# Third block's mixer: the attention projection split by heads, a joint root for the layer norm, and heads normalized from one clipped and scaled sum

## The chip, the cores and the metric

One core of a Trainium2 chip runs the whole program. The metric is device microseconds of one execution, the median over runs. TensorE (PE) multiplies, VectorE (DVE), ScalarE (ACT) and GpSimd (POOL) work on tiles of 128 partitions, and SyncE's queue (SP) starts the loads of weights. Every engine works through its own instructions in the order in which they were written, and waits at semaphores for the others.

## The reference

Three blocks run one after another on x of 512 tokens by 1024 features. The change touches only the mixer of the third:

```
h = rms_norm_3(x, mix_norm)
g_a, g_b, z_uv, z_q, z_k, z_v = split(h @ w_in)          # 6144 columns
# branch a: u, v = gelu(z_uv); v = layer_norm(v) * gain + bias (over 512 features, eps 1e-5)
#           y_a = u * (masked 128x128 product of v by chunks + b_s)
# branch b: 8 heads of two query/key parts of 64 and a value of 128
q, k = partial_rope(rms_norm(q)), partial_rope(rms_norm(k))
a = softmax(q1 k1) - lam * softmax(q2 k2)                # causal, blocks of 128 queries
o = rms_norm_3(a @ v, subln) * (1 - lam_init)            # over the head's 128 features, eps 1e-6
m = sigmoid(g_a) * (y_a @ a_w_proj) + sigmoid(g_b) * (y_b @ b_w_proj)
x = x + m @ w_out
```

Around it lie the two gated feed-forward layers of the block. All of it is float32 in precision.

## The kernel before

**Layout.** Activations are kept with features on partitions: a tile `t(i)` is 128 features by 512 tokens. A projection is made of "dense" groups: one group gives 128 output features and runs over its input's k steps (8 for 1024 features). Each k step is three matmuls of 128x128 by 128x512, since weights and inputs are carried as two rounded parts: high by high, high by low, low by high (L863 to L865). A weight panel (up to 8 k steps) is loaded by SP to one of three buffers `W`, its high part is copied by ACT and its low part subtracted by POOL (`split`, L2231 and L2612) into one of four buffers `R`. Inputs are split to two parts likewise by `pair`: ACT copies the high part (L2266), DVE subtracts to the low one (L1484).

**Order.** The order of all steps is a list, `ORDER`, made before the program is written. Each engine's function walks it and issues its own part of each step. Where many small chains run beside projections, `merge(chains, *fills)` builds the list: it keeps a planned clock for each engine from the costs in `SEG`, takes a chain's step as soon as its predecessors (`AFTER`) are planned to be done by the time PE is free, and otherwise takes the next two k steps of a fill. Of several fills the first whose input or tile is free (`room`) is taken. A group once begun is finished before another is opened. A projection's result lies in one of two banks of PSUM in merged stretches, in one of seven in the stretches marked `wide`.

**The mixer of the third block before** (`order`, from L617). After norm 5 come the four `v` tiles of branch a (`gv`, and `gvt`, their transposes to tokens on partitions). Then the three input tiles of head 0 and the three of head 1 are put in the list, outside the merge. Then a merge of three chains: heads 0, 2, 4, 6; heads 1, 3, 5, 7 (`diff_head`); and branch a (`mlp`): per token block m a mean and centering (`gn`, DVE, with ACT's square and sum), then its root and scaling (`gn2`), then four `gu` tiles with `gs` and `pair`. The fills are the inputs of heads 2 to 7, and `rest`: gate tiles of branch a with `a_proj`, and gate tiles of branch b. Inputs of heads 2 and 3 need branch a finished, those of head h from 4 on need head h-4 normalized. Head h starts once head h-2 is normalized (`slot_free`).

A head: transpose v, squares of q and k, token sums on PE (L874), a root of Newton steps on DVE (`newton`, L1378 to L1391), spreads on PE (L888), scaling (L2033, L2036), rotation (`fr`, PE L1354 and L1356, DVE L2172 to L2175), then four query blocks: scores L1314, maximum L2050, exponent L2521, the difference of the two softmaxes L2073 and L2075, transposes L1323, product with v L1332. Its ending is `ft1` to `ft3`: ACT copies the output (L2583); DVE makes a clipped copy and one scaled by 2^-70 (L2185, L2186), ACT squares both, PE sums both over features with a matrix of ones (L1361, L1363), DVE joins the two sums, adds eps and takes the reciprocal (L2197 to L2202), ACT takes the root (L2595), DVE applies a mask and scales the output (L2208, L2210).

After the merge: eight pairs of the heads' outputs, then `b_proj` over all eight k steps of each of 8 groups, each followed by `branch` on DVE (gate times product L1816, add to m L1820), the pairs of m, and `out3` (evicted at L1517) with the next norm's work.

## Time and profile before

| | |
|---|---|
| median of 3 runs | 3356.03 us (3352.72 to 3356.92) |
| the profiled execution's time | 3356.43 us |
| its span, first to last instruction | 3354.6 us |
| PE busy | 3159.9 us, 94% |
| DVE, ACT, POOL busy | 1646.1, 1047.7, 1160.5 us (49%, 31%, 35%) |
| DMA | 22.6% of 16 engines, 74 GB/s |

A profile is one execution. Busy shares are means over the span, so each reading starts from a stretch: what it holds, who is busy in it, and what PE waited for. A window's row gives, after its bounds and length, the busy microseconds of each engine with the number of instructions, then the granted clock of PE as a share of full speed, and the DMA. The mixer of the third block lies between 2400 and 3000 us of the span.

### The profile page before, as it was taken

The page shows a single profiled execution, that of the slowest core. Times are in us where ns is not written, and L with a number is a line of the kernel's source. Part 1 is how long each engine was busy: PE and PEld are TensorE (multiplying, and loading weights), DVE is VectorE, ACT ScalarE, POOL GpSimd, SP SyncE. Part 2 cuts the span into 40 slices and gives each one's busy share as a digit, 9 for nine tenths or more (in the row PEclk, how much of TensorE's full clock was granted, in tenths as well). Part 3 has the DMA queues.
Part 4 walks back from the last instruction along what each step waited for, and adds up shares of the span by engine and source line. Part 5 has one row for each costly group of instructions (what it writes and reads, how often), then busy time and mean ns, then how long its engine had stood idle before and what let it go on. Part 6 is the DMA issues. An engine that isn't in the chain of part 4 may idle for free.

```text
span 3354.6 us, 40426 instructions
## 1 busy us (share of the span) xinstructions
PE 3159.9 (94%) x16604; PEld 2589.4 (77%) x16604; DVE 1646.1 (49%) x3287; ACT 1047.7 (31%) x1691; POOL 1160.5 (35%) x542
## 2 busy tenths in 40 slices
PE   7989999998999898999999989999788999899999
PEld 5768888897888786867877768888666777678887
DVE  4865656454577416557674343331337576443310
ACT  3342223222322223223223333232224334332221
POOL 2442333333444342213212334444322223334443
PEclk9998999999999999999999989999899999899999
DMA  3211111112244331012011222233211112223232
GB/s 113 82 45 38 57 45 63 57 45 72 98 152 144 115 99 54 21 37 67 22 39 49 75 66 94 96 98 99 86 57 55 54 59 73 65 80 100 95 101 88
DMA packets 71480, 247.88 MB, mean 74 GB/s; under 512 B 8064, under 2 KB 8448, under 8 KB 71168
## 3 DMA queue, kind: packets, MB, share of 16 engines
q1 hardware_dynamic: 71296, 245.30, 22.6%
q8 instruction: 131, 2.15, 0.3%
q14 instruction: 53, 0.43, 0.0%
HBM read 243.18 MB, written 2.10 MB: 73 GB/s over the span
## 4 chain that ended last, share of the span: by engine, by line
PE 86%; DVE 11%; ACT 2%; issue 1%; POOL 0%; DMA 0%; SPq 0%; DVEq 0%; ACTq 0%
PE bank L863 22%; PE bank L865 22%; PE bank L864 22%; PE bank L903 7%; PE bank L874 2%; PE bank L897 1%; PE bank L1314 1%; PE bank L881 1%; PE bank L1332 1%; PE bank L888 1%; PE bank L1323 1%; DVE u L1484 1%; DVE sm L1389 0%; PE bank L1160 0%; PE bank L1208 0%
## 5 line engine op out<-in xcount | busy, mean ns | idle before, releaser
L2612 POOL TENSOR_TENSOR R<-W,R 128x1024 fp32r<-128x1024 f32 (+2 forms) x448 | 1050.1, 2348 | 1960.4 <-ACT R L2231 1960.4
L863 PE MATMUL bank<-u,R 128*128 128x512 f32 (+1 forms) x3440 | 1391.8, 405 | 43.3 <-issue 12.4
L865 PE MATMUL bank<-u,R 128*128 128x512 f32 (+1 forms) x3440 | 1355.4, 394 | 0.0
L864 PE MATMUL bank<-u,R 128*128 128x512 f32 (+1 forms) x3440 | 1355.0, 394 | 0.0
L863 PEld LDWEIGHTS bank<-u,R 128*128 128x128 f32 (+1 forms) x3440 | 655.1, 190 | 199.7 <-issue 39.9
L865 PEld LDWEIGHTS bank<-u,R 128*128 128x128 f32 (+1 forms) x3440 | 652.9, 190 | 143.6 <-issue 0.8
L864 PEld LDWEIGHTS bank<-u,R 128*128 128x128 f32 (+1 forms) x3440 | 655.1, 190 | 130.2 <-issue 3.3
L2231 ACT ACTIVATE R<-W 128x1024 fp32r<-128x1024 f32 (+2 forms) x448 | 450.4, 1012 | 197.9 <-PE bank L865 194.8
L903 PE MATMUL bank<-t,t 128*128 128x128 f32 x2000 | 238.8, 276 | 3.5 <-DVE t L1700 1.0
L903 PEld LDWEIGHTS bank<-t,t 128*128 128x128 f32 x2000 | 233.3, 192 | 10.3 <-DVE t L1676 1.8
L2266 ACT ACTIVATE u<-t 128x512 fp32r<-128x512 f32 x126 | 76.3, 627 | 291.7 <-DVE t L1506 246.2
L1517 DVE SCALAR_TENSOR_TENSOR X<-bank,X 128x512 f32<-128x512 f32 x32 | 22.1, 692 | 260.3 <-PE bank L865 260.3
L1492 DVE TENSOR_TENSOR t<-bank,t 128x512 f32<-128x512 f32 x66 | 45.5, 690 | 171.5 <-PE bank L865 158.9
L1484 DVE TENSOR_TENSOR u<-t,u 128x512 fp32r<-128x512 f32 x126 | 98.5, 804 | 51.5 <-ACT u L2266 51.3
L2273 ACT ACTIVATE t<-t 128x512 f32<-128x512 f32 x66 | 41.7, 633 | 243.3 <-DVE t L1492 243.2
L874 PEld LDWEIGHTS bank<-CN,t 128*128 128x128 f32 x672 | 92.3, 213 | 25.5 <-issue 9.4
L874 PE MATMUL bank<-CN,t 128*128 128x1 f32 (+1 forms) x672 | 89.2, 261 | 17.1 <-ACT t L2238 8.0
L1506 DVE TENSOR_TENSOR t<-t,bank 128x512 f32<-128x512 f32 x66 | 45.4, 687 | 120.3 <-PE bank L865 118.6
L1528 DVE SCALAR_TENSOR_TENSOR t<-bank,sm,t 128x511 f32<-128x511 f32 (+2 forms) x108 | 80.8, 748 | 46.5 <-ACT t L2282 43.9
L2638 POOL TENSOR_TENSOR t<-t,CN 128x512 f32<-128x512 f32 x40 | 51.8, 1297 | 114.9 <-PE bank L903 114.8
L2521 ACT ACTIVATE t<-t,sm 128x128 f32<-128x128 f32 (+3 forms) x96 | 53.9, 561 | 116.8 <-DVE sm L2053 116.7
L1816 DVE SCALAR_TENSOR_TENSOR t<-t,bank 128x512 f32<-128x512 f32 x48 | 33.0, 687 | 105.7 <-PE bank L865 105.6
(368 smaller groups left out, 2844.1 us busy)
## 6 DMA issues: line engine op xcount, KB each, us to landing
W<-in_in SPq DMA_DIRECT2D x48, 512.0 KB, 3.3
W<-in_ff_in SPq DMA_DIRECT2D x44, 512.0 KB, 3.4
W<-in_g_qkv SPq DMA_DIRECT2D x24, 512.0 KB, 3.3
W<-in_ada SPq DMA_DIRECT2D x24, 512.0 KB, 3.5
W<-in_f1g SPq DMA_DIRECT2D x22, 512.0 KB, 3.3
W<-in_f1u SPq DMA_DIRECT2D x22, 512.0 KB, 3.3
W<-in_f2g SPq DMA_DIRECT2D x22, 512.0 KB, 3.3
W<-in_f2u SPq DMA_DIRECT2D x22, 512.0 KB, 3.3
```

Source lines behind the costliest of these rows:

```text
L863: e.matmul(b[0:cols, :], wh, hi, start=(k == 0), stop=False)
L864: e.matmul(b[0:cols, :], wh, lo, start=False, stop=False)
L865: i = e.matmul(b[0:cols, :], wl, hi, start=False, stop=(k == KT - 1))
L874: i = e.matmul(b[:, m * n:m * n + n], x[:, m * 128:m * 128 + 128], one, start=first and m == 0, stop=last and m == 3, skip_group_check=True)
L903: i = e.matmul(b[:, s], l[:, s], x[:, s], start=True, stop=True)
L1484: e.tensor_tensor(r(lo[k]), t(src[k]), r(hi[k]).bitcast(F32), SUB).then_inc(*PR.dve.up("lo", tag, k))
L1528: e.scalar_tensor_tensor(out=c[:, s:512], in0=b[:, 0:512 - s], scalar=half(wname, (3 - s) * nt + gj), in1=c[:, s:512], op0=MUL, op1=ADD).t ...
L2231: e.activation(R[q % NH][:, 0:n], W[p % NW][:, 0:n], ACT.Copy).then_inc(*PN.act.up("hi", key))
L2266: e.activation(r(hi[k]), t(src[k]), ACT.Copy).then_inc(*PR.act.up("hi", tag, k))
L2521: e.activation(ex, ex, ACT.Exp, bias=c[:, 0:1], scale=0.125, accum_out=c[:, 1:2]).then_inc(*AT.act.up("exp", u, m, qb))
L2612: e.tensor_tensor(R[q % NH][:, 1024:1024 + n], W[p % NW][:, 0:n], R[q % NH][:, 0:n].bitcast(F32), SUB).then_inc(*PN.pool.up("lo", key))
L2638: e.tensor_tensor(v3(t(V_.d)), v3(t(V_.L)), C(f"q{16 << n}").unsqueeze(1).broadcast_to([128, 4, 128]), MUL).then_inc(*IV.pool.up("q", v, n))
```

## The change

**Order.** The inputs of heads 0 and 1 go from the fixed list into the first fill. The layer norm's four means, centerings and squares come first, then one root for all four token blocks (`gnn` on four columns), then four scalings. `b_proj` becomes two projections: `b_proj` with the first six heads' six k steps, whose groups are added to the end of `rest` and so fill in the merge, and `b_proj2` with the last two heads' two k steps, after the merge. A new chain of the merge makes the pairs of heads 0 to 5, once head h is normalized and all 48 tiles of the input projection have been opened.

**Adds.** A group of `b_proj` is multiplied by its gate into a spare tile and added to m by DVE (`part`). A group of `b_proj2` is multiplied by its gate on DVE, and the add to m moves to POOL (`branch` in the POOL function). The pair of m number j-2 follows group j.

**Ending of a head.** One copy clipped at 2^65, squared with a scale of 2^-32, summed once, eps and reciprocal, root, then one operation that tests the sum against a limit and multiplies, and the scaling (heads 0 to 5). Heads 6 and 7 (`fc1` to `fc4`) sum to a column per token, run Newton's steps on 128x4 and spread the root by PE.

The planner's costs `SEG` follow. The core of the diff:

```diff
-    "b_proj": (8, 8, 128), ...
+    "b_proj": (8, 6, 128), "b_proj2": (8, 2, 128), ...
+LIMIT = 2.0 ** 64 * (1 - 2.0 ** -22)
+PT = (66, 67)
-    "ydiff": (YD, H0, H1),
+    "ydiff": (YD[0:6], H0[0:6], H1[0:6]),
+    "ydiff2": (YD[6:8], H0[6:8], H1[6:8]),
-    ft1="s.6 v1.5", ft1s="s1.2", ft1p="p1.7", ft2="v6.5", ft2r="s.63", ft3="v1.44", ...
-    gn="v1.63 s.81", gn2="v5.26", ...
+    ft1="s.6 v.5", ft1s="s.63", ft1p="p.9", ft2="v4.1", ft2r="s.63", ft3="v1.44", fc1="p.9", fc2="v3.0", fc3="p.9", fc4="v.74", ...
+    gn="v1.33 s.81", gnn="v2.4", gn2="v1.4", ...
+                              "ydiff": [("ft3", k)] + [opens("in3", j) for j in range(48)], ...
+    if name == "b_proj":
+        return [("pair", "ydiff", h) for h in range(6)]
-    return out + [("ft1", h), ("ft1s", h), ("ft1p", h), ("ft2", h), ("ft2r", h), ("ft3", h)]
+    return out + [("ft1", h), ("ft1s", h)] + [(k, h) for k in (("ft1p", "ft2", "ft2r", "ft3") if h < 6 else ("fc1", "fc2", "fc3", "fc4"))]
-    O += attention_in(("f", 0)) + attention_in(("f", 1))
-    mlp = [x for m in range(4) for x in (("gn", m), ("gn2", m))]
+    mlp = [("gn", m) for m in range(4)] + [("gnn",)] + [("gn2", m) for m in range(4)]
-    O += merge([[s for h in range(a, 8, 2) for s in diff_head(h)] for a in range(2)] + [mlp],
-               sum([attention_in(("f", h)) for h in range(2, 8)], []), rest)
-    O += [("pair", "ydiff", h) for h in range(8)]
-    O += wide(gated("b_proj", "in3", 8, GG3, M3, False))
-    O += [("pair", "m3", j) for j in range(8)] + wide(residual("out3", 6))
+    rest += [s for j in range(8) for s in tiles("b_proj", j, ("part", "b_proj", j, "in3", 8 + j, GG3[j], M3[j]))]
+    O += merge([[s for h in range(a, 8, 2) for s in diff_head(h)] for a in range(2)] + [mlp, [("pair", "ydiff", h) for h in range(6)]],
+               sum([attention_in(("f", h)) for h in range(8)], []), rest)
+    O += [("pair", "ydiff2", h) for h in range(2)]
+    last = [tiles("b_proj2", j, ("branch", "b_proj2", j, "in3", 8 + j, GG3[j], M3[j])) + [("pair", "m3", j - 2)] * (j > 1) for j in range(8)]
+    O += wide(sum(last, []) + [("pair", "m3", 6), ("pair", "m3", 7)] + residual("out3", 6))
```

On the engines (PE, DVE, ACT and POOL in this order):

```diff
             def ft1p(h):
-                e.matmul(bank[q.X], C("ones"), t(q.et[0]), start=True, stop=True).then_inc(*DF.pe.up("oc", h))
-                e.matmul(bank[q.Y], C("ones"), t(q.et[1]), start=True, stop=True).then_inc(*DF.pe.up("od", h))
+                e.matmul(bank[q.Y], C("ones"), t(q.e[0]), start=True, stop=True).then_inc(*DF.pe.up("sum", h))
+            def fc1(h):
+                token_sum(bank[q.Y], t(q.e[0]), 1, True, True).then_inc(*DF.pe.up("sum", h))
+            def fc3(h):
+                spread(bank[q.X], parts[q.parts][:, 0:4], parts[q.parts][:, 4:8]).then_inc(*DF.pe.up("rb", h))
+            def part(name, j, gname, gj, x, m):
+                e.scalar_tensor_tensor(out=s, in0=t(x), scalar=1.0, in1=bank[BANK[name, j]], op0=ADD,
+                                       op1=MUL).then_inc(*BR.dve.up("got", name, j))
+                e.tensor_tensor(t(m), t(m), s, ADD).then_inc(*BR.dve.up("part", name, j))
+            def gnn():
+                w.wait_ge(*GM.act.at("var", 3))
+                e.tensor_scalar(c[:, 8:12], c[:, 4:8], 1.0 / 512, 1e-5, MUL, ADD).then_inc(*GM.dve.up())
+                newton(GM.dve, c[:, 8:12], c[:, 12:16], c[:, 16:20], c[:, 20:24])
             def gn2(m):
-                w.wait_ge(*GM.act.at("var", m))
-                e.tensor_scalar(c[:, 2:3], c[:, 1:2], 1.0 / 512, 1e-5, MUL, ADD).then_inc(*GM.dve.up())
-                newton(GM.dve, c[:, 2:3], c[:, 3:4], c[:, 4:5], c[:, 5:6])
             def ft1(h):
-                e.tensor_scalar(t(q.e[0]), o, 1e18, -1e18, MIN, MAX).then_inc(*DF.dve.up("oc", h))
-                e.tensor_scalar(t(q.e[1]), o, 2.0 ** -70, None, MUL).then_inc(*DF.dve.up("od", h))
+                e.tensor_scalar(t(q.e[0]), t(YD[h]), 2.0 ** 65, -2.0 ** 65, MIN, MAX).then_inc(*DF.dve.up("oc", h))
             def ft2(h):
-                after(e.tensor_scalar(oc, bank[q.Y], 2.0 ** -12, None, ALU.is_lt))
-                after(e.tensor_scalar(od, bank[q.Y], 2.0 ** -12 * (1 - 2.0 ** -22), 2.0 ** 70, MIN, MUL))
-                after(e.tensor_scalar(od, od, 2.0 ** 70, None, MUL))
-                after(e.tensor_tensor(od, od, bank[q.X], MAX))
-                after(e.tensor_scalar(r_, od, 1.0 / 128, 1e-6, MUL, ADD))
-                after(e.reciprocal(r_, r_), "rec", h)
+                e.tensor_scalar(t(q.q), bank[q.Y], 1.0 / 128, 1e-6 * 2.0 ** -64, MUL, ADD).then_inc(*DF.dve.up())
+                e.reciprocal(t(q.q), t(q.q)).then_inc(*DF.dve.up("rec", h))
             def ft3(h):
-                e.tensor_tensor(r_, r_, oc, MUL).then_inc(*DF.dve.up())
+                e.scalar_tensor_tensor(out=r_, in0=bank[q.Y], scalar=LIMIT, in1=r_, op0=ALU.is_lt, op1=MUL).then_inc(*DF.dve.up())
             def ft1s(h):
-                e.activation(t(q.et[0]), t(q.e[0]), ACT.Square).then_inc(*DF.act.up("oc", h))
-                e.activation(t(q.et[1]), t(q.e[1]), ACT.Square).then_inc(*DF.act.up("od", h))
+                e.activation(t(q.e[0]), t(q.e[0]), ACT.Square, scale=2.0 ** -32).then_inc(*DF.act.up("sq", h))
+            def branch(name, j, gname, gj, x, m):
+                if name == "b_proj2":
+                    w.wait_ge(*BR.dve.at("part", "b_proj", j))
+                    w.wait_ge(*BR.dve.at("got", name, j))
+                    e.tensor_tensor(t(m), t(m), t(x), ADD).then_inc(*BR.pool.up("m", name, j))
```

## Rows read from the trace of the kernel before

**Rows 1.** Busy time by stretch; columns as named in its first line
```profile
core 0: us, PE busy (x) PEld busy (x) DVE busy (x) ACT busy (x) POOL busy (x), PEclk, DMA share, GB/s
2447.20:2484.20 37.00, 37.00 (x174) 30.78 (x172) 1.33 (x3) 13.73 (x25) 14.61 (x6) 1.00 0.26 86
2484.20:2545.00 60.80, 40.84 (x228) 30.00 (x229) 47.82 (x171) 16.60 (x39) 7.16 (x3) 0.75 0.08 27
2545.00:2875.90 330.90, 319.16 (x1666) 244.51 (x1662) 210.25 (x518) 142.86 (x275) 95.71 (x43) 0.99 0.20 62
2875.90:2894.60 18.70, 3.86 (x5) 1.17 (x4) 14.72 (x17) 6.41 (x11) 0.00 (x0) 0.59 0.01 3
2894.60:2942.90 48.30, 46.14 (x192) 37.72 (x192) 15.86 (x25) 14.57 (x21) 20.64 (x8) 0.95 0.27 88
2942.90:2950.50 7.60, 7.56 (x25) 5.61 (x26) 6.33 (x7) 0.95 (x2) 2.94 (x1) 0.78 0.20 69
```

**Rows 2.** The page's part 4, chain that ended last, by engine
```profile
PE 86%; DVE 11%; ACT 2%; issue 1%; POOL 0%; DMA 0%; SPq 0%; DVEq 0%; ACTq 0%
```

**Rows 3.** Waits of PE, 2484.2 to 2545: total us, times, longest us
```profile
PE bank L1314 <- DVE t L2175: 8.7, 2, 5.7
PE bank L1323 <- DVE t L2075: 7.6, 2, 7.1
```

**Rows 4.** Waits of PE, 2545 to 2875.9
```profile
PE bank L1323 <- DVE t L2075: 6.3, 8, 2.0
```

**Rows 5.** Waits of PE, 2875.9 to 2950
```profile
PE bank L863 <- issue: 9.4, 1, 9.4
PE bank L1361 <- ACT t L2588: 5.5, 1, 5.5
```

**Rows 6.** DVE: timeline at 2484, and two groups of 2484.2 to 2545
```profile
2484.22 0.15 DVE L2109 TENSOR_SCALAR sm<-sm 128x1 f32<-128x1 f32 x1 [34.77 <-ACT t L2561]
...
L1389 DVE SCALAR_TENSOR_TENSOR sm<-sm 128x1 f32<-128x1 f32 (+1 forms) x18 | 5.0, 279 | 0.6
...
L2100 DVE TENSOR_REDUCE sm<-t 128x1 f32<-128x512 f32 x3 | 2.0, 680 | 0.0
```

**Rows 7.** Groups of DVE, 2545 to 2900: busy us, mean ns, idle before
```profile
L2202 DVE RECIPROCAL t<-t 128x512 f32<-128x512 f32 x8 | 26.8, 3352 | 0.3
...
L2197 DVE TENSOR_SCALAR t<-bank 128x512 f32<-128x512 f32 x8 | 5.5, 690 | 17.5 <-PE bank L1363 17.4
```

**Rows 8.** Timeline of PE from 2881: start, us, what
```profile
2881.44 2.07 PE L1361 MATMUL bank<-t,CN 128*128 128x512 f32 x2 [5.46 <-ACT t L2588]
...
2894.65 0.77 PE L863 MATMUL bank<-u,R 128*128 128x512 f32 x1 [9.43 <-issue]
...
2899.79 0.39 PE L863 MATMUL bank<-u,R 128*128 128x512 f32 x1
```

**Rows 9.** Timeline: even heads normalized (L2210), last products copied (L2583)
```profile
2598.51 0.75 DVE L2210 SCALAR_TENSOR_TENSOR t<-t,PC,t 128x512 f32<-128x512 f32 x1
...
2669.86 0.60 ACT L2583 ACTIVATE t<-bank 128x512 f32<-128x512 f32 x1 [1.47 <-PE bank L1332]
...
2694.82 0.75 DVE L2210 SCALAR_TENSOR_TENSOR t<-t,PC,t 128x512 f32<-128x512 f32 x1
...
2770.36 0.59 ACT L2583 ACTIVATE t<-bank 128x512 f32<-128x512 f32 x1
...
2789.90 0.75 DVE L2210 SCALAR_TENSOR_TENSOR t<-t,PC,t 128x512 f32<-128x512 f32 x1
```

**Rows 10.** POOL's splits from 2360 on by form; POOL and DVE at 2944
```profile
L2612 POOL TENSOR_TENSOR R<-W,R 128x1024 fp32r<-128x1024 f32 x126 | 306.3, 2432 | 526.6 <-ACT R L2231 526.6
...
L2612 POOL TENSOR_TENSOR R<-W,R 128x512 fp32r<-128x512 f32 x8 | 10.7, 1339 | 54.8 <-ACT R L2231 54.8
...
2943.93 2.94 POOL L2612 TENSOR_TENSOR R<-W,R 128x1024 fp32r<-128x1024 f32 x1 [10.29 <-ACT R L2231]
...
2944.57 4.66 DVE L1484 TENSOR_TENSOR u<-t,u 128x512 fp32r<-128x512 f32 x4
```

## Prediction: which waits go, and what comes in their place

> **What bounds the kernel now.** I read four views, from coarse to fine. The chain of work that ended last comes first: TensorE (PE) makes 86% of it and VectorE (DVE) 11% [rows 2]. So removing work from another engine buys nothing unless PE stood waiting for it. I cut the third block's mixer by stage, from the end of the layer norm's transposes (2447.2) to the eviction of the output projection's first tile (2950.5), and compare length with PE's busy time [rows 1]. Two stages stick out. In 2484.2 to 2545.0 PE is busy 40.84 of 60.80 us at a granted clock of 0.75; in 2875.9 to 2894.6 it is busy 3.86 of 18.70 at 0.59. The long stretch between is 96% busy (319.16 of 330.90).
>
> The waits say who is late there. In the first stage PE waits 8.7 us for the rotated keys and 7.6 us for the softmax products, both DVE work [rows 3]. DVE itself had idled 34.77 us before its first operation of the layer norm's root [rows 6]: that root needs ScalarE's square, and ScalarE's queue holds it behind the copies of six projection tiles which the order puts first. Then the four roots, two heads' roots and both rotations come at once, and the only fill left for PE is one gate tile. At the end PE waits 5.5 and 9.4 us while heads 6 and 7 are normalized, with no matmul left to fill in [rows 5].
>
> **The ledger of what can go.** First stage: 60.80 - 40.84 = 19.96 us idle. Besides, PE is slow after it stood: behind the tail's last wait twelve full-width matmuls take 5.14 us, 0.43 each, where 0.23 is normal (1.2 and 2.4 GHz) [rows 8]. Behind this stage's two long waits there are seven and nine such matmuls, 16 x 0.2 = 3.2 us, 3.5 with the heads' own. Together 23.5. Tail: 18.70 - 3.86 = 14.84 idle, and head 7's first ones-matmul took 2.07 us where 0.43 x 2 is normal; with the second I count 2.0 more: 16.9 [rows 8]. The projection stage: 48.30 - 46.14 = 2.2 idle and the twelve slow matmuls, 5.14 - 12 x 0.227 = 2.4: 4.6. The first tile after it ends 0.3 us before the 7.60 us window does, in place of after 24 x 0.227 = 5.4: 1.8 [rows 1]. Sum 46.8 us.
>
> **PE work.** Per head 0 to 5 one of two ones-matmuls goes: half of the four passes of 0.43 us, 0.86 us, times six = 5.1 us. Heads 6 and 7 exchange theirs for 4 one-column sums and 8 narrow spreads, which I take as even. The b_proj matmuls are as many as before (64 k steps of three, 43.6 us), only 48 of them go forward as eight pieces of 4.1 us and 16 (10.9 us) stay behind. PE work from 2447.2 to the end of the first output tile was 503.0 - 46.8 - 11.7 (idle of the long stretch, which I leave in place) = 444.5, and becomes 439.4.
>
> **The joint root and the moved projections.** Four roots of 14 small operations at 0.15 to 0.28 us [rows 6] become one: some 42 instructions, 8 us of DVE. What matters more is their place. DVE does the four means and centerings (a reduce of 0.68 [rows 6] and two shorter steps each, 5.3 us), one root (14 small steps, 2.5) and four scalings (two full-width steps of about 0.7 each, 5.8), some 14 to 16 us with ScalarE's squares, while PE runs the three tiles of head 0, 3 x 5.44 = 16.3 us. So the layer norm is hidden as it ends, with 0 to 2 us to spare; what follows are the branch's four `gu` tiles, then the rest. If that cover fails the wait is the difference: I take 2 us, bounds 0 and 5 (a first score cannot be asked before its tiles, but other tiles are ready).
>
> The price is that head 1 starts late. Before it come head 0's three tiles (16.3), one of its own (5.4), four `gu` tiles (21.8), two of its own (10.9) and some 10 us of head 0's matmuls: 2447.2 + 64.4 = 2511.6. On the even side a head takes 71.4 and 75.0 us from the moment its slot is free (the head before it normalized) to the copy of its last product, mean 73, and then 25.7 and 20.3, mean 23, to its normalized output [rows 9]. The operations of that ending add up to 12.8 us; the change takes away a full-width multiply, a square, a ones-matmul and four or five of DVE's full-width steps of 0.4 to 0.7 us, and keeps the reciprocal of 3.35 [rows 7]. That leaves 8.7. Scaled as the waits scale now, 23 becomes about 17. The odd heads then end at 2511.6 + 4 x 73 + 3 x 17 = 2855, with head 7's short ending (no reciprocal, small operations) 2865. All of PE's work before the last piece, b_proj's six-head pieces in it, lasts until 2447.2 + 439.4 - 10.9 - 5.4 + 2 + 11.7 = 2884. So work is left when the last head ends, and the tail wait goes. The slack of 19 us is no more than the scatter of two heads; I price the remaining tail at 4 us, bounds 0 and 20.
>
> Do the fills reach until b_proj may start? It needs head 5 normalized, about 2511.6 + 3 x 73 + 3 x 17 = 2782. By then PE has 335 us, of which 14 go to waits and some 105 to heads (439.4 less the fills' 261, b_proj's 43.6 and the output tile's 5.4 is 129 for eight heads, and six and a half are through), so 216 of fills are used; 44 tiles of 5.44 and a_proj's 21.8 make 261. They reach.
>
> **The last two heads' piece.** PE needs 10.9 us for it, GpSimd (POOL) more. Each of the eight columns wants a new add on POOL and the split of a 256-column panel, and during the last ones the panels of the output projection. The add I take at the price of a 512-wide subtract, 1.34 us, since no plain add of this kernel runs there in these stages; a 1024-wide split is 2.43 [rows 10], so a 256-wide one is 0.8 by the slope between the two. POOL needs 1.35 + 0.8 + hops 0.2 = 2.35 us for a column, where PE needs 1.36. In order: column 7's split stands behind five adds and five splits, 14 us after the stage begins; then come three adds with two full splits between, 9.5 us; then pair 7 on ScalarE and DVE (1.7) and its k step (0.7). The first output tile ends after 26 us, where PE alone needs 16.3: 9.7 us new. DVE's full-width subtracts wait where POOL runs: four of them took 4.66 us while POOL's split took 2.94, so one of them about 2.6 us in place of 0.69 [rows 10]. If each of eight columns paid 0.69 again it would be 15. I take 12, bounds 6 (a short wait hides behind the k steps) and 15. DVE's extra 8 multiplies (0.69 each, 5.5 us) lie beside PE work in the long stretch; without that cover they would be 5.5.
>
> The Trainium skill, page "SBUF — State Buffer", section "Who interferes with whom", says that a DVE instruction with two SBUF inputs and a GpSimd instruction that reads SBUF exclude each other for the whole instruction. By that rule, which speaks against moving the adds to POOL, this stage costs 15 in place of 9.7 and the sum is 3327 against 3322; the stretched subtract agrees with it.
>
> **DMA and other queues.** b_proj is loaded in 16 smaller panels, 8 of 384 KB and 8 of 128 KB. SyncE's queue holds only loads, and three buffers are fetched ahead; DMA is 27% busy or less in these stages [rows 1]. I cost it at nothing; if the short panels came late, up to 3 us of the stage, inside its bound. Slow clock after new waits: 1.5 us.
>
> **Sum.** Gone 46.8 + 5.1 = 51.9; new 2 + 4 + 12 + 1.5 = 19.5; net 32.4. The profiled execution took 3356.43 (span 3354.6), the median of the runs is 3356.03, so its time stands for both: 3356.4 - 32.4 = 3324.0.
>
> **Rivals.** (a) The odd heads are late. If a head takes 80 us and an ending 20, the odd chain ends at 2511.6 + 320 + 60 + 10 = 2902, PE's work at 2884, and a tail wait of some 18 us takes the place of 4: 3338 (3334 to 3342). For it: the even heads' own figures differ by 4 us a head and 5 an ending, and the chain has four of each. Against: the endings are shorter, and DVE has less to do. (b) Slower: the last head runs alone. If all fills, b_proj's pieces included, run out 43 us before head 7 ends, that tail and the 15.5 of other new costs eat the 51.9 and another 6.7. A head's own matmuls are only about 16 us of its 73, so a tail of 50 gives 3356.4 - 51.9 + 15.5 + 50 = 3370. That needs the odd chain to end at 2884 + 43 = 2927 or later in place of 2865, two thirds of a head late. (c) The change does not what it says: the start's waits (23.5) move by 30 us and stay, and the last piece costs 15: 51.9 - 23.5 - 22.5 = 5.9, so 3350.5. Against it: the tiles of head 0 are ready at 2447.2 whatever the planner does. (d) More than forecast: the 11.7 us idle in the long stretch, more than half of it behind DVE's softmax products [rows 4], shrink to half, and the tail wait is nil: 3314.
>
> **How the numbers follow.** Forecast 3324 with chance 0.60 (own range 3314 to 3334), (a) 0.20, (b) 0.06, (c) 0.06, (d) 0.08. Bounds: all new costs at their lower end and half the long stretch's idle gone, 3305; at the upper end (5 + 20 + 15, and 4 for the clock), 3348. The range 3306 to 3345 leaves out (b), (c) and what lies beyond the bounds. A measurement of this kernel tells 0.2% (6.7 us) from no change. Faster 0.87, same 0.06, slower 0.07.
>
> **What would show it.** Right: DVE starts the root within 15 us of 2448; the stage from 2484 to 2545 is over 95% busy on PE at clock 1.0; head 1's first copy to heads stands near 2510; b_proj pieces between 2820 and 2885; less than 8 us idle there; POOL back to back for some 20 us in the last piece. Wrong: PE idle over 10 us before the last piece; a last piece with first tile longer than 32 us; a long stretch with 20 us idle; or a gain found outside the mixer.

## The result

The changed kernel takes 3319.62 us (3317.68 to 3321.77) where the kernel before takes 3354.38 in the same rounds: ratio 0.9898, 95% interval 0.9886 to 0.9911, 34.8 us less. The forecast was 3324.0. The profiled execution took 3317.71 us, its span is 3315.8; PE is busy 3140.3 us (95%, from 94%), DVE 1638.5, ACT 1044.1, POOL 1174.5.

The profile of the changed kernel by the stages that were cut before [rows 1]; the mixer begins some 4.5 us earlier in this execution, so the stretches are moved by that much. The last is the last two heads' piece with the first output tile.

```profile
core 0: us, PE busy (x) PEld busy (x) DVE busy (x) ACT busy (x) POOL busy (x), PEclk, DMA share, GB/s
2443.00:2480.00 37.00, 37.00 (x210) 30.66 (x209) 28.72 (x51) 14.06 (x27) 14.36 (x6) 1.00 0.22 72
2480.00:2540.00 60.00, 56.79 (x315) 43.30 (x314) 34.44 (x81) 25.11 (x44) 17.11 (x7) 0.97 0.19 62
2540.00:2842.00 302.00, 289.01 (x1526) 222.20 (x1524) 179.26 (x497) 131.31 (x257) 85.16 (x39) 0.99 0.19 61
2842.00:2886.80 44.80, 38.14 (x173) 31.24 (x174) 27.25 (x50) 13.11 (x25) 14.07 (x9) 0.96 0.15 45
2886.80:2912.60 25.80, 19.82 (x73) 14.01 (x73) 17.05 (x17) 9.45 (x15) 21.82 (x16) 0.93 0.36 112
```

The stretch behind the layer norm, 40.84 of 60.80 us busy at clock 0.75 before, is now 56.79 of 60.00 busy at 0.97. DVE does its share beside PE: 28.72 us in the first row, where it had 1.33. Two stages have gone: the 18.70 us in which PE did almost nothing, and the projection of 48.30 us, of which only the 25.80 us of the last row stand apart. The chain that ended last has shifted from DVE, 11% in [rows 2], to 9%:

```profile
PE 86%; DVE 9%; ACT 2%; POOL 1%; issue 1%; DMA 0%; SPq 0%; DVEq 0%; ACTq 0%; POOLq 0%
```

What PE waits for in the changed kernel: first 2443 to 2545, then 2840 to 2886.9, then 2886.9 to 2913 (total us, times, longest).

```profile
PE bank L1334 <- DVE t L2110: 2.1, 1, 2.1
PE bank L899 <- DVE sm L1410: 1.1, 1, 1.1
...
PE bank L874 <- issue: 3.9, 1, 3.9
PE bank L892 <- DVE sr L1444: 2.2, 1, 2.2
PE bank L874 <- DVE t L1846: 2.2, 1, 2.2
...
PE bank L874 <- POOL R L2658: 4.8, 5, 2.4
PE bank L874 <- DVE t L1851: 0.8, 1, 0.8
```

At the start 3.2 us of waits are left, where PE stood idle for 19.96 us before (60.80 - 40.84 in [rows 1]; the two waits of [rows 3] are 16.3 of it). In the tail 8.3 stand where [rows 5] has 14.9: 3.9 for the pairs of six heads, made in one burst once the merge's conditions are met, 2.2 for head 7's root, 2.2 for the pairs of heads 6 and 7, which stand on DVE behind the last `part`. In the last piece PE waits five times for POOL's splits (L2658).

**The measure used below.** A median of this kernel carries what happens in the 2440 us ahead of the mixer, whose code is the same. So beside the medians I compare the *stage*: from DVE's first reduction of the layer norm to the eviction of the first output tile. It is 2448.1 to 2950.55 us of the span before, 502.45 us, and 2443.6 to 2912.78 after, 469.18 us: 33.3 less, so nearly all of the gain lies in the mixer. One profile per kernel stands behind each such length; its scatter, as a pair of kernels below shows, is about 4 us. Ratios are to the kernel before in the same rounds; in the four sets of rounds that kernel took 3354.38 (after), 3356.19 (e1 to e4), 3357.84 (e5, e6, e7, e10) and 3358.58 us (e8, e11, e13, e15), so medians of different sets are compared to some 4 us at best.

| kernel | median us | ratio, 95% | stage us | PE idle in it | last products of heads 0, 1 / 6, 7 copied, us into the stage |
|---|---|---|---|---|---|
| before | 3354.38 | | 502.5 | 48.8 | 126.0, 126.9 / 415.1, 426.5 |
| after | 3319.62 | 0.9886-0.9911 | 469.2 | 28.8 | 91.9, 135.8 / 364.5, 414.7 |
| e15_order_only | 3334.92 | 0.9906-0.9945 | 479.7 | 33.3 | 103.6, 130.0 / 392.8, 404.8 |
| e5_ending_only | 3335.51 | 0.9925-0.9961 | 479.3 | 33.2 | 126.0, 127.0 / 388.8, 399.5 |
| e7_split_only | 3356.13 | 0.9987-1.0009 | 502.9 | 49.4 | 126.0, 127.0 / 415.2, 426.7 |
| e6_start_only | 3366.69 | 1.0022-1.0052 | 513.4 | 56.6 | 91.9, 141.6 / 401.5, 443.6 |
| e2_four_roots | 3315.43 | 0.9859-0.9888 | 457.4 | 20.9 | 103.5, 123.8 / 369.2, 379.8 |
| e1_order_back | 3332.33 | 0.9911-0.9941 | 482.8 | 36.7 | 116.2, 117.1 / 384.6, 395.2 |
| e3_old_ending | 3355.73 | 0.9985-1.0009 | 504.8 | 50.1 | 91.8, 141.5 / 403.6, 461.7 |
| e4_no_split | 3322.79 | 0.9881-0.9920 | 474.4 | 30.7 | 91.9, 135.8 / 366.2, 406.6 |
| e8_add_dve | 3320.77 | 0.9869-0.9918 | 473.5 | 28.9 | 91.8, 135.7 / 366.2, 416.6 |
| e10_head1_first | 3313.63 | 0.9864-0.9899 | 460.6 | 21.6 | 112.6, 134.0 / 376.0, 377.8 |
| e11_head1_pairs | 3308.03 | 0.9831-0.9866 | 458.5 | 17.5 | 111.2, 133.0 / 362.5, 372.1 |
| e13_four_pairs_mixed | 3304.99 | 0.9822-0.9862 | 455.0 | 15.6 | 103.7, 124.5 / 389.7, 391.6 |

### The profile page after: what moved, and what is told of

Read it like the earlier page. It is cut to its first block, busy times and chain, and to the rows that moved or that the text cites. A ratio compares the mean times of both kernels' runs of the same rounds, so it can differ in the third digit from the quotient of the medians.

```text
span 3315.8 us, 40438 instructions
## 1 busy us (share of the span) xinstructions
PE 3140.3 (95%) x16616; PEld 2576.8 (78%) x16616; DVE 1638.5 (49%) x3243; ACT 1044.1 (31%) x1689; POOL 1174.5 (35%) x558
## 3 DMA queue, kind: packets, MB, share of 16 engines
q1 hardware_dynamic: 72448, 245.30, 23.1%
## 4 chain that ended last, share of the span: by engine, by line
PE 86%; DVE 9%; ACT 2%; POOL 1%; issue 1%; DMA 0%; SPq 0%; DVEq 0%; ACTq 0%; POOLq 0%
PE bank L874 22%; PE bank L876 22%; PE bank L875 22%; PE bank L914 7%; PE bank L885 2%; PE bank L908 1%; PE bank L892 1%; PE bank L1325 1%; PE bank L1343 1%; PE bank L899 1%; DVE u L1507 1%; PE bank L1334 1%; POOL R L2658 1%; DVE sm L1408 0%; PE bank L1171 0%
## 5 line engine op out<-in xcount | busy, mean ns | idle before, releaser
L2658 POOL TENSOR_TENSOR R<-W,R 128x1024 fp32r<-128x1024 f32 (+3 forms) x456 | 1053.3, 2314 | 1900.3 <-ACT R L2279 1900.3
L2279 ACT ACTIVATE R<-W 128x1024 fp32r<-128x1024 f32 (+3 forms) x456 | 452.1, 998 | 201.6 <-PE bank L876 195.1
L885 PE MATMUL bank<-CN,t 128*128 128x1 f32 (+1 forms) x688 | 90.2, 259 | 17.6 <-ACT t L2286 8.6
```

Source lines behind the costliest of these rows:

```text
L885: i = e.matmul(b[:, m * n:m * n + n], x[:, m * 128:m * 128 + 128], one, start=first and m == 0, stop=last and m == 3, skip_group_check=True)
L2279: e.activation(R[q % NH][:, 0:n], W[p % NW][:, 0:n], ACT.Copy).then_inc(*PN.act.up("hi", key))
L2658: e.tensor_tensor(R[q % NH][:, 1024:1024 + n], W[p % NW][:, 0:n], R[q % NH][:, 0:n].bitcast(F32), SUB).then_inc(*PN.pool.up("lo", key))
```

## The experiments: one part taken out of the change

The forecast's ledger adds independent terms. If that is right, each part, undone alone, gives its term back. The first four runs do that.

**The tiles of heads 0 and 1 back ahead of the merge.**

```diff
+    O += attention_in(("f", 0)) + attention_in(("f", 1))
     mlp = [("gn", m) for m in range(4)] + [("gnn",)] + [("gn2", m) for m in range(4)]
...
-               sum([attention_in(("f", h)) for h in range(8)], []), rest)
+               sum([attention_in(("f", h)) for h in range(2, 8)], []), rest)
```

> The changed kernel, but the six input tiles of heads 0 and 1 stand before the merge again; joint root, endings and split stay. Theory (the gain at the start is one of order: ScalarE's squares and with them DVE's root waited behind the copies of those tiles): a burst of DVE work returns after 2480, shorter than before by the three roots (8 us); PE waits 10 to 15 us there with 2 to 4 us of slow clock. Against the changed kernel (3319.6) plus 12 to 18 us: 3332 to 3338. Rival (the three saved roots are the gain, the place of the tiles is not): plus 0 to 5 us.

Measured: the stage is 13.7 us longer, and the 60 us behind its first 40 are busy 42.39 at clock 0.78, as in the kernel before. PE waits 17.6 us there for DVE, a little more than expected, and the median of 3332.33 lies at the lower edge of the range. The mechanism of the start is as forecast; its worth here is 13.7, not 21.5.

**Four separate roots in place of the joint one.**

```diff
-    gn="v1.33 s.81", gnn="v2.4", gn2="v1.4", gs="p.88 v1.38").items()}
+    gn="v1.63 s.81", gn2="v5.26", gs="p.88 v1.38").items()}
...
-    mlp = [("gn", m) for m in range(4)] + [("gnn",)] + [("gn2", m) for m in range(4)]
+    mlp = [x for m in range(4) for x in (("gn", m), ("gn2", m))]
...
```

> The changed kernel, but each token block has its own root again, between its centering and its scaling; the input tiles of heads 0 and 1 stay in the fill. Theory (DVE has idle time while PE runs these tiles): the 8 us more of DVE are hidden, plus 0 to 3 us against the changed kernel. Rival (the joint root counts by its own length): plus 8 us or more.

Measured: the stage is 11.8 us *shorter*, 457.4, and the median 4.2 us lower (6.0 when each is taken against the kernel before of its own rounds; the two intervals just touch). Some 40 more small operations on DVE cost nothing that can be seen, and the change to a joint root, held to be free, costs 11.8. That missed every theory. The planner's costs go with the root in this edit, so the order of PE's list changes too; the section on the joint root takes that up.

**The old ending of the heads** (clipped and scaled copies, two squares, two sums, for all eight heads).

```diff
-    return out + [("ft1", h), ("ft1s", h)] + [(k, h) for k in (("ft1p", "ft2", "ft2r", "ft3") if h < 6 else ("fc1", "fc2", "fc3", "fc4"))]
+    return out + [("ft1", h), ("ft1s", h), ("ft1p", h), ("ft2", h), ("ft2r", h), ("ft3", h)]
```

> The changed kernel with the old ending of all eight heads (two copies, two squares, two ones-matmuls, six DVE steps); order, joint root and split stay. Theory: PE does 5.1 us more, and each ending is some 6 us longer, so the odd heads end 20 us or so later, of which the slack of b_proj's pieces hides a part: plus 5.1 and a tail of 3 to 15 us, 3328 to 3340. Rival (chains are not near the end of PE's work, only the matmuls count): plus 5 us, 3325.

Measured: 35.7 us more, all of the gain gone (ratio 0.9997). Far beyond both.

**One whole attention projection after the merge.**

```diff
-    "b_proj": (8, 6, 128), "b_proj2": (8, 2, 128),
+    "b_proj": (8, 8, 128),
...
-    O += [("pair", "ydiff2", h) for h in range(2)]
-    last = [tiles("b_proj2", j, ("branch", "b_proj2", ...
+    O += [("pair", "ydiff", h) for h in range(8)]
+    O += wide(gated("b_proj", "in3", 8, GG3, M3, False))
```

> The changed kernel with b_proj whole after the merge, pairs of all eight heads before it and adds on DVE, as before the change; order, joint root and endings stay. Theory: nothing fills while heads 6 and 7 end, so PE waits 15 to 20 us with 4 us of slow clock, but the last piece's POOL waits (9 us) and the changed kernel's own waits around its pieces (8 us) go: plus 5 to 15 us, 3325 to 3335. Rival (the split is the main part of the gain): plus 17 us or more.

Measured: 5.3 us more in the stage, 3.2 in the median, hardly above the scatter. The terms given back add up to 13.7 - 11.8 + 35.7 + 5.3 = 42.9, not to 33.3. They are not independent, so I turned the question round.

## The experiments: one part alone on the kernel before

**The short endings alone** (order, four roots and whole projection as before).

> The kernel before with the shorter endings of the heads alone (one copy, one square, one ones-matmul, three DVE steps for heads 0 to 5; the narrow root for 6 and 7). Length of the mixer means here and below the time from DVE's first reduce of the layer norm to the first eviction of the output projection: 502.5 before, 469.2 after. Ledger theory (as predicted): 5.1 us of PE and the shorter last ending, minus 10 to 14: length 488 to 492. Chain theory (each ending is paid three times over in the chain of four heads, and DVE is shared by two chains): minus 18 to 26: length 476 to 484.

Measured: 479.3, 23.1 us less. The forecast's price for the endings was 5.1 us of PE work. PE's busy time falls 7.5 (453.7 to 446.2), its idle time 15.6. The tail shows where; PE's waits from 2852 to 2932:

```profile
PE bank L871 <- DVE t L1852: 2.2, 1, 2.2
PE bank L871 <- issue: 2.0, 1, 2.0
PE bank L889 <- DVE sr L1441: 0.6, 1, 0.6
```

4.8 us, where [rows 5] has 14.9 and, with the same wait of 2.2 us for the last add to m, 17.1 stood. From the copy of a head's last product to its normalized output the first six heads take 15.8 us on average, 23.6 before. Three such endings lie on the way to head 7, whose last product comes 27 us earlier (3 x 7.8 = 23.4 of it), and PE still has other work when it ends. So the tail wait belongs to the endings: no pieces of the projection were needed to fill it.

**The moved tiles and the joint root, without the rest.**

> The kernel before with the start alone: input tiles of heads 0 and 1 in the fill and the joint root. Ledger theory: minus 23 us, length 479. Chain theory: the start's waits go, but head 1 starts late and the long endings make the odd heads end late, with nothing left to fill, so the tail wait grows by as much: minus 0 to 8, length 495 to 502.

Measured: 513.4. The start has no wait (56.78 of 60 us busy), and yet the kernel is *slower* than before, ratio 1.0037 (1.0022 to 1.0052). Both theories missed.

**The split alone.**

> The kernel before with the split of b_proj alone (pieces of six heads as fill, last piece with POOL's adds). Both theories: b_proj's pieces fill the 19 us of the last endings, the last piece costs 9 us on POOL: minus 8 to 14, length 488 to 495. Rival: the pieces come too late or take PE from the heads: minus 0 to 4.

Measured: no change, 502.9. In the ledger it was to bring the filled tail and projection stage. PE's timeline where the pieces begin:

```profile
2876.99 0.39 PE L877 MATMUL bank<-u,R 128*128 128x512 f32 x1
2886.35 0.77 PE L875 MATMUL bank<-u,R 128*128 128x512 f32 x1 [8.96 <-issue]
```

By then every other fill is used up, so the pieces, which need all six pairs, wait for the pairs. Those stand on DVE behind head 6's reciprocal and head 7's two copies, and then come in one burst; PE goes on 2.4 us into it:

```profile
2878.25 3.35 DVE L2247 RECIPROCAL t<-t 128x512 f32<-128x512 f32 x1
...
2883.95 5.31 DVE L1510 TENSOR_TENSOR u<-t,u 128x512 fp32r<-128x512 f32 x6
```

9.0 us of wait stand there in place of 9.4 [rows 5], behind another matmul. What the pieces fill is paid back by POOL's waits in the last piece (4.8 us). The split is not worth nothing everywhere: with the moved tiles, the joint root and the old endings, where the heads end late, the stage is 513.4 without it (e6) and 504.8 with it (e3), and with the short endings 474.4 (e4) and 469.2.

**The moved tiles alone, with four roots.** This tells the two halves of the slower kernel apart.

> The kernel before, with the tiles of heads 0 and 1 moved into the ordered merge and nothing else: four separate roots, the long ending of the heads, one whole attention projection. The forecast gave this move nearly all of its 23.5 us at the start of the stage: 502.5 less 20 gives 482. With the joint root as well, the same move made the stage 11 us longer than before (513.4), and in the other pair of kernels the joint root alone cost 11.8 (469.2 against 457.4). Theory A (the chain of odd heads sets the end, and the joint root is what delays it): the first four heads come as in the kernel with four roots (104, 124, then some 8 us later per head for the long ending), and the stage is 13.4 minus 11.8, that is 498 to 505 us, no gain although the start wait of 20 us is gone. Rival B (the forecast's ledger): 480 to 486. Rival C (the long ending is the fault whatever the root): over 508.

Measured: 479.7, 22.8 us less; 3334.92 us. The forecast's ledger (rival B here) was right, and my chain theory, which blamed the old endings, fell. It is the change to a joint root, with the list that comes of it, that turns the gain of 22.8 into a loss of 11.0: 33.7 us with the old endings, 11.8 with the new. Of the 33.7, 23.3 are idle time of PE (56.6 against 33.3) and the rest longer busy time at a lower granted clock.

## What the joint root does

It makes the first 100 us no slower. These are the windows of the kernel with the tiles moved and four roots, from 2452.1 (first 100 us of the stage, next 300, the rest):

```profile
2452.10:2552.10 100.00, 96.86 (x534) 76.44 (x533) 74.33 (x197) 42.64 (x78) 31.65 (x13) 0.98 0.21 69
2552.10:2852.10 300.00, 288.25 (x1510) 220.69 (x1508) 190.19 (x491) 128.91 (x254) 86.13 (x39) 0.99 0.19 62
2852.10:2931.80 79.70, 61.34 (x237) 46.65 (x237) 39.67 (x50) 22.54 (x32) 23.93 (x9) 0.83 0.18 60
```

and with the joint root besides, from 2442.7:

```profile
2442.70:2542.70 100.00, 96.78 (x538) 76.20 (x537) 66.59 (x140) 39.16 (x68) 31.44 (x13) 0.98 0.21 69
2542.70:2842.70 300.00, 282.75 (x1458) 217.27 (x1457) 193.28 (x454) 128.22 (x242) 86.24 (x39) 0.98 0.19 62
2842.70:2956.10 113.40, 77.30 (x286) 55.37 (x285) 53.88 (x102) 33.59 (x57) 23.95 (x9) 0.76 0.13 42
```

PE's waits of this last row, in the same kernel:

```profile
PE bank L1330 <- DVE t L2108: 15.4, 3, 7.2
PE bank L870 <- issue: 9.4, 1, 9.4
```

15.4 us for the softmax products of the late heads, with nothing left to fill in. Head 7 comes late, at 443.6. With the short endings, four roots (e2) and then the joint root (the changed kernel), PE's idle time differs by 7.9 us, and most of that lies in the 300 us behind the first 100:

```profile
2554.80:2854.80 300.00, 291.34 (x1562) 225.80 (x1561) 178.03 (x505) 129.15 (x257) 87.15 (x41) 1.00 0.18 60
...
2543.60:2843.60 300.00, 285.41 (x1509) 219.51 (x1507) 176.35 (x490) 132.31 (x260) 85.16 (x39) 0.99 0.19 60
```

What differs is the *phase* of the two chains. With four roots the last products of an even and an odd head come in pairs, 11 to 26 us apart; with the joint root they alternate, 42 to 53 us apart (changed kernel: 43 to 50, at 91.9, 135.8, 181.1, 224.4, 272.8, 321.1, 364.5, 414.7 us). And where the chains alternate, an ending takes longer:

| kernel | last products of two heads of a pair, us apart | us per head, odd chain | of these up to the last product + ending | mean ending, heads 0 to 5 |
|---|---|---|---|---|
| four roots, short endings (e2) | 11 to 20 | (379.8 - 123.8) / 3 = 85.3 | 69.2 + 16.1 | 17.9 |
| joint root, short endings (after) | 43 to 50 | (414.7 - 135.8) / 3 = 93.0 | 69.4 + 23.6 | 23.2 |
| four roots, old endings (e15) | 12 to 26 | (404.8 - 130.0) / 3 = 91.6 | 68.0 + 23.6 | 23.0 |
| joint root, old endings (e6) | 42 to 53 | (443.6 - 141.6) / 3 = 100.7 | 70.6 + 30.0 | 30.0 |
| tiles ahead, joint root, short endings (e1) | 1 to 23 | (395.2 - 117.1) / 3 = 92.7 | 76.7 + 16.0 | 16.6 |
| tiles ahead, four roots, short endings (e5) | 1 to 23 | (399.5 - 127.0) / 3 = 90.8 | 75.7 + 15.1 | 15.8 |

In the first two rows the odd chain's own endings account for 7.5 of the 7.7 us between them, in the next two for 6.4 of 9.1. All fourteen kernels agree on the endings: with short ones 15.1 to 17.9 us where the heads come in pairs and 23.2 to 23.7 where they alternate, with the old ones 23.0 to 23.6 and 30.0. The length of a whole head is not set by the phase alone. In the last two rows heads 0 and 1 start together, their endings are short, and yet a head takes 91 to 93 us, because the part ahead of the ending takes 76.

The timeline of the changed kernel shows what an ending stands behind. Head 2's last product is copied while head 3 is in its rotation and first query blocks (ACT, then DVE, then ACT):

```profile
2624.73 0.60 ACT L2631 ACTIVATE t<-bank 128x512 f32<-128x512 f32 x1 [0.29 <-PE bank L1343]
...
2625.59 0.69 DVE L2211 TENSOR_TENSOR t<-bank,t 128x512 f32<-128x512 f32 x1 [2.90 <-PE bank L1365]
...
2629.71 0.69 DVE L2214 TENSOR_TENSOR t<-t,t 128x512 f32<-128x512 f32 x1
2630.32 0.42 DVE L2223 TENSOR_SCALAR t<-t 128x512 f32<-128x512 f32 x1
...
2633.59 0.19 ACT L2569 ACTIVATION_READ_ACCUMULATOR t<-t,sm 128x1 f32 x1
2633.69 0.62 ACT L2636 ACTIVATE t<-t 128x512 f32<-128x512 f32 x1
```

The clipped copy (L2223) needs only the line above all, done at 2625.3, and starts at 2630.32, behind six steps of head 3's rotation (L2211 to L2214) that come first in DVE's list. The square (L2636) could follow at 2630.7 and starts at 2633.69, behind two of head 3's exponentials, the first of which had waited for DVE (L2088). Eight of the 23 us of this ending pass so. Nothing of it is a wait that PE's list would show.

Why the chains alternate can be read from `ORDER`. With the joint root the planner reckons the layer norm done earlier, and puts the four `gu` tiles of branch a (21.8 us of PE) ahead of head 1's q and k tiles; with four roots they stand behind all three tiles of head 1. So head 0, alone on the engines, gets ahead (91.9 in place of 103.5) and head 1 falls back (135.8 in place of 123.8).

Is it the phase, or only that head 1 starts late? One line of the order holds the `gu` tiles back until head 1's inputs have been opened; the joint root stays. PE's list then has the tiles of heads 0 and 1 and the `gu` tiles in the same order as with four roots.

```diff
     if name == "in3" and 16 <= j < 20:
-        return [("gn2", 3)]
+        return [("gn2", 3), opens("in3", 33)]
```

> The changed kernel, with the four gu tiles of branch a held back until head 1's inputs are opened. Chain theory (head 1 starts 20 us late behind them, and never makes it up): the odd heads end 15 to 25 us earlier, PE becomes the bound, minus 8 to 14 us against the changed kernel, length 455 to 461. Rival (the four roots were faster for another reason, such as fewer waits at ScalarE): no change, length 467 to 471.

Measured: 460.6, 8.6 us less. Head 1's last product comes at 134.0, hardly before the 135.8 of the changed kernel, and head 0's is 21 us *later*. But the chains now run in pairs, the odd one takes (377.8 - 134.0) / 3 = 81.3 us a head in place of 93.0, and head 7's last product comes 36.9 us earlier. So a late head 1 is not the fault. That the phase is what lengthens the endings is what all the kernels and the queue lines agree on; it is not shown by a run that changed the phase and nothing else, since the order of the fills moves with it. This run also tells the root from its list: with the joint root kept and the tiles in the other order the stage is 460.6, with four roots 457.4. So by these profiles 8.6 of the 11.8 us belong to the place of the `gu` tiles, and the 3.2 left for the root itself are within the scatter.

The stage wins only 8.6 of those 36.9 us. Behind head 7's normalized output it still lasts 70.3 us, with PE busy in 59.2 of them, where it lasts 42.6 in the changed kernel: PE's own work (439.0 us in all, 21.6 idle) now sets most of the end.

## The last piece, and a better version

**The eight adds on DVE in place of POOL.**

```diff
-                return [BR.pool.at("m", "b_proj2", k)]
+                return [(BR.pool if k < 0 else BR.dve).at("m", "b_proj2", k)]
...
-                if m is not None and name != "b_proj2":
+                if m is not None and not (name == "b_proj2" and j < 0):
...
```

No j or k is below 0, so all eight adds go to DVE.

> The changed kernel, with the eight additions of the last piece of the attention projection done by VectorE in place of GpSimd; nothing else differs. In the changed kernel's profile GpSimd is busy 21.8 of the last piece's 25.8 us, TensorE waits 4.8 us there for its splits, and VectorE's pair subtractions last 1.2 to 2.2 us beside the additions where they last 0.69 elsewhere. Theory A (GpSimd and the memory that it shares with VectorE cost what the forecast set aside, 12 us for the whole last piece): without the additions the splits come at once, VectorE's steps shorten, and the stage of 469.2 us loses 3 to 7 us. Rival B (VectorE is then the late one, with eight more steps of 0.7 us): the stage stays within 2 us of 469.2. Everything ahead of the last piece is the same to 0.1 us under both, and the median, which scatters by some 6 us from code that is unchanged, says little of either.

Measured, in the piece's own row: with its first tile it takes 26.6 us (2900.46 to 2927.06) where the changed kernel takes 26.2, although POOL's busy time in it falls from 22.0 to 10.7; DVE's rises from 17.3 to 20.9:

```profile
2900.46:2927.06 26.60, 21.35 (x73) 16.02 (x74) 20.94 (x26) 9.23 (x15) 10.71 (x7) 0.83 0.33 107
```

Nearer to theory B, with one reservation: the granted clock was 0.83 in this piece and 0.93 in the changed kernel's, so PE was busy 1.1 us longer in it (21.35 against 20.20) and stood idle 0.7 less. So POOL's adds are not what bounds this piece alone. The stage is 4.3 longer all the same, and 3.9 of that arise before the piece, where both kernels give PE the same instructions in the same order and the lengths were expected to agree within 0.1 us. This is the scatter of a single profile that I reckon with, and by it the 5.3 us of the undivided projection are hardly a difference.

**Pairs formed as the heads end**, into tiles that are free early, on top of the reordered `gu` tiles:

```diff
-    "ydiff": (YD[0:6], H0[0:6], H1[0:6]),
+    "ydiff": (YD[0:6], (56, 58, 68, 70, 42, 45), (57, 59, 69, 71, 43, 46)),
...
-                              "ydiff": [("ft3", k)] + [opens("in3", j) for j in range(48)], ...
+                              "ydiff": [("ft3", k), ("pair", "yg", 3)], ...
```

> The kernel that gave 460.6 us for the stage (head 1's inputs opened ahead of the gate's tiles), and the pairs of heads 0 to 5 written into tiles that are free early, so that each is formed when its head ends and not in one burst, and the pairs of heads 6 and 7 inside the merge. In the changed kernel TensorE waits 3.9 us for that burst and 2.2 us ahead of the last piece. Theory A (the tail's waits are now what is left): the stage loses 4 to 8 us more, 453 to 457. Rival B (the end is TensorE's work, 439 us of the 460.6, and the heads' chain holds no more): the waits move elsewhere, 459 to 462.

Measured: 458.5, 2.1 less and within the scatter; the median is 5.6 lower. It stands nearer to rival B. PE's waits before the last piece are gone, and what is left from 2840 to 2910 is the split, with 1.2 us more in two short waits for DVE:

```profile
PE bank L873 <- POOL R L2657: 4.8, 5, 2.4
```

**Four roots, early pairs, and three of the eight adds on POOL.**

> The changed kernel with four separate roots in place of the joint one (that alone gave a stage of 457.4 us), the early pairs as in the kernel before this one, and of the eight additions of the last piece three left on GpSimd (odd tiles up to 5), the others on VectorE. Theory A (root, pairs and additions each cost what the runs and waits show: 11.8, 4 to 6, and 3 to 5): 448 to 453 us for the stage, a median of some 3307. Rival B (not additive, since TensorE is busy 436.5 of the 457.4 us and only 20.9 are idle): 454 to 458, a median of 3313 to 3317.

Measured: 455.0, 2.4 below the kernel with four roots alone: rival B. PE is busy 439.4 of it. At 3304.99 us, ratio 0.9842 (0.9822 to 0.9862), it beats both kernels, the changed one by 14.6 us. In the stage 11.8 of its 14.2 us come with the root taken apart; of the medians that step accounts for only 4.2 of 14.6. And the kernel that keeps the joint root but holds the `gu` tiles back, with the early pairs (e11), is within the scatter of it: 458.5 us and 3308.03.

## Why the prediction was right, and where it was not

The total was right within 4.4 us of the median (in the stage: 33.3 measured, 32.4 forecast). That it came so close is in part luck: three terms were better than forecast, by 1.3, 5.1 and 6.7 us, and the one that was put at nothing cost 11.8. Its terms, set beside the parts run alone:

| step of the forecast | forecast | measured |
|---|---|---|
| start of the stage: 23.5 gone, 2 new | -21.5 | -22.8 (e15) |
| endings and tail: 5.1 + 16.9 gone, 4 new | -18.0 | -23.1 (e5) |
| split: 4.6 + 1.8 gone; 12 + 1.5 new | +7.1 | +0.4 alone (e7); -5.3 to 0 in the change |
| joint root: hidden | 0 | +11.8 (e2), +33.7 with old endings |
| sum | -32.4 | -33.7 (with the root at 11.8 and the split at +0.4) |

The first three and four roots should give 502.5 - 22.8 - 23.1 + 0.4 = 457.0; the kernel that is just that measured 457.4. So the ledger's parts do add up there, where the chains run in pairs; with the joint root they do not (42.9 against 33.3 when each is taken out). Point by point:

- *Start of the stage.* Right that it is hidden, with one step mis-sized. DVE's root began 9 us after the stage did (within 15 was wanted), but the four scalings ended at 2466.3, 22.7 us after the first reduction and not 14 to 16: three steps lasted 2.3 to 2.9 us beside a split on POOL, one of them a 128x4 step that takes 0.17 elsewhere. Head 0's three tiles (16.3 us) would not have covered that; the first tile of head 1, which the list has there too, did.

```profile
2452.32 1.38 DVE L2144 TENSOR_SCALAR sm<-sm 128x4 f32<-128x4 f32 x1 [1.53 <-ACT t L2609]
...
2455.96 2.29 DVE L1408 SCALAR_TENSOR_TENSOR sm<-sm 128x4 f32<-128x4 f32 x1
...
2455.84 2.39 POOL L2658 TENSOR_TENSOR R<-W,R 128x1024 fp32r<-128x1024 f32 x1 [2.17 <-ACT R L2279]
```

  The stretch behind it is 95% busy (56.79 of 60.00) at 0.97, just short of the over 95% at 1.0 that was wanted.
- *"The joint root and the moved projections."* Here a step failed. Its 8 us on DVE are indeed hidden. But I looked only at the delay of head 1 that follows (its input was forecast for 2511.6, less 4.5 for the earlier start; its q tile was copied at 2508.74) and took it as harmless while work for PE is left. What I did not see is that the chains get out of step, and that the endings then stand longer in DVE's and ScalarE's lists for the rest of the stage.
- *Length of a head.* "A head 73, an ending 17": 90 together, and measured 88.6 to 96.7. (The rows give 70.6 and 74.8 us from a normalized head to the next copy, not 71.4 and 75.0; the mean of 73 stands.) But that is two errors that cancel: the ending is 23.2, as before, not 17, and the part ahead of it is 66 to 73, mean 69, not 73. The end of the odd chain was put at 2850 in this execution's time and head 7's last product was copied at 2858.32: 8 late. The slack of 19 covered it. With rival (a), odd heads late, the tail has 8.3 us of waits in place of the 4 taken.
- *PE work and the tail.* 5.1 us of ones-matmuls against 7.5 less busy in e5: right in kind. That a shorter ending counts three times in a chain was used to place the end, and not to ask which part empties the tail. I gave the tail to the fills; the endings alone empty it. The pieces of `b_proj` begin at 2844.3, inside the 2820 to 2885 of the forecast.
- *The last two heads' piece.* 26 by the rows, 28.3 with the 12 I took: measured 26.2, so the 9.7 computed from the rows were right (9.9 by the row) and the added stretches too dear. The steps fit as well: the last 256-wide split ends 14.0 us into the piece, and three adds with two full splits take 9.8 more, where 14 and 9.5 were forecast. The stretches are there. In the changed kernel DVE's pair of 0.69 us lasts 1.82 beside POOL's add, and a split of 0.73 lasts 1.18 (POOL, then DVE):

```profile
2890.34 0.73 POOL L2658 TENSOR_TENSOR R<-W,R 128x256 fp32r<-128x256 f32 x1
...
2898.17 1.28 POOL L2691 TENSOR_TENSOR t<-t,t 128x512 f32<-128x512 f32 x1
2899.42 1.18 POOL L2658 TENSOR_TENSOR R<-W,R 128x256 fp32r<-128x256 f32 x1
...
2898.18 1.82 DVE L1507 TENSOR_TENSOR u<-t,u 128x512 fp32r<-128x512 f32 x1
...
2911.03 0.69 DVE L1507 TENSOR_TENSOR u<-t,u 128x512 fp32r<-128x512 f32 x1 [1.85 <-ACT u L2314]
```

  DVE stands idle a third of the piece, so I take it that its longer steps end in time; no run shows that by itself. The Trainium skill, page "SBUF — State Buffer", section "Who interferes with whom", has these two instructions exclude each other; the trace agrees in that both get longer, but the 15 us that I worked out by it did not come.
- *Rivals.* (a) came in part, as said. (b), the last head alone, did not come, but its mechanism shows in e6: 15.4 us of waits in the tail behind a long odd chain, and a kernel slower than before. With the short endings put back in (e4) the stage falls from 513.4 to 474.4. (c) did not come. (d)'s halved idle time in the long stretch did not come either: 302.00 - 289.01 = 13.0, from 11.7.

## What to carry to other kernels

Where two chains of small steps share engines with fixed lists, look at their phase and not only at their lengths: when the same step of each chain ends (here the copies of the last products), and what an ending stands behind in its own engine's list, not only at what the bound engine waits for. A saving in a step that every link of such a chain repeats is worth its length times the links on the way to the end, up to the point where the bound engine's own work takes over. Where a planner builds the list from costs, a step made cheaper moves other steps: print the list before and after, since here four tiles in front of head 1 cost more than the saved root could give. A forecast that is right in the sum can be errors that cancel, so run each part both alone and as the one left out: the joint root was the only part that cost, and either taking it out or moving the four tiles back gave a faster kernel.

## What was not expected of the hardware

Unchanged code does not take the same time in every execution of a program: the stage began at 2442.7 to 2455.3 us of the span over these kernels, whose code up to there is the same. Part of it is in the first 100 us. From 60 to 80 us, in the changed kernel and then in the one with the adds on DVE:

```profile
60.00:80.00 20.00, 19.98 (x94) 16.69 (x95) 15.32 (x19) 8.50 (x15) 7.20 (x3) 1.00 0.31 103
```

The other:

```profile
60.00:80.00 20.00, 18.85 (x82) 15.70 (x83) 14.59 (x22) 7.63 (x14) 7.13 (x3) 0.91 0.25 79
```

94 matmuls at full clock against 82 at 0.91. Of the fourteen profiles five have 1.00 in this window, and there the stage begins at 2442.7 to 2449.4; the others have 0.83 to 0.91, and 2446.9 to 2455.3. What sets the clock back there was not tried. Differences of medians under some 5 us between two of these kernels were therefore read with the stage beside them.
